# One gather of 8 KB per expert in place of two of 4 KB, in a hybrid encoder with product-key experts

## The reference

```python
def one_block(hb):                                   # 128 tokens
    q = (hb @ w_query).reshape(t, 8, 2, 128)         # 8 heads, two halves
    s = einsum('thpc,phkc->thpk', q, keys)           # 128 keys per half
    sv, si = top_k(s, 16)                            # 16 best of each half
    ...                                              # 256 sums, the 16 best of them
    idx  = ...                                       # 8 x 16 = 128 experts per token
    gate = softmax(top_s)
    u = expert_u[idx]                                # 128 rows of 1024 per token
    act = gelu(einsum('tnd,td->tn', u, hb))
    return einsum('tn,tnd->td', gate * act, expert_v[idx])
```

## Time and profile before

| | us |
|---|---|
| median of 3 runs | 3242.87 |
| lowest and highest run | 3241.06, 3247.12 |
| the profiled execution: its time | 3239.72 |
| its span, first to last instruction | 3237.8 |

### The profile page before, as it was taken

The page is one execution under the profiler, slowest core; times in us unless marked ns, Lnnn a source line. Parts: engine busy times, 40 slices in busy tenths (PEclk is TensorE's granted clock), DMA queues, the critical chain, the costliest instruction groups (busy, mean ns, idle before and its releaser), DMA issues.

```text
span 3237.8 us, 29913 instructions
## 1 busy us (share of the span) xinstructions
PE 2408.2 (74%) x5786; PEld 1028.4 (32%) x5796; DVE 2227.9 (69%) x5353; ACT 465.2 (14%) x1379; POOL 2073.9 (64%) x2147
## 2 busy tenths in 40 slices
PE   7999986876677567756677677767776777766557
PEld 3575342332233223323233233323332333222113
DVE  1123178897679867975689669866887679866663
ACT  1126211111111111101111111111111111111000
POOL 0000125677777777767767777777777777777775
PEclk9999998998899999989998989988998899888999
DMA  3121148999999999999999999999999999999999
GB/s 105 52 112 57 33 130 315 388 396 398 409 409 405 396 407 409 401 408 408 409 379 399 401 401 409 376 401 401 408 376 401 401 409 410 408 402 399 409 410 364
DMA packets 319943, 1134.32 MB, mean 350 GB/s; under 512 B 37825, under 2 KB 42945, under 8 KB 317793
## 3 DMA queue, kind: packets, MB, share of 16 engines
q0 software_dynamic: 299520, 1090.65, 85.6%
q1 hardware_dynamic: 20320, 42.62, 3.6%
HBM read 1130.97 MB, written 2.10 MB: 350 GB/s over the span
## 4 chain that ended last, share of the span: by engine, by line
DMA 24%; issue 20%; DVE 17%; PE 14%; POOL 6%; DVEq 1%; ACT 1%; POOLq 0%; ACTq 0%
DMA v_ring<-in_peer_v,idx_v 21%; PE psum L1370 12%; DVE u_ring L1462 4%; DMA u_ring<-in_peer_u,idx_u 3%; POOL u_ring L1339 3%; POOL v_ring L1351 3%; DVE hres L1454 2%; DVE work L1101 1%; PE psum L975 1%; DVE si L1117 1%; DVE si L1099 1%; DVE sv L1126 1%; DVE tpos L1099 1%; DVE sv L1111 1%; DVE tpos L1117 1%
## 5 line engine op out<-in xcount | busy, mean ns | idle before, releaser
L1370 PE MATMUL psum<-v_ring,w_col 128*128 128x512 f32 x3136 | 1681.8, 673 | 760.3 <-DMA v_ring<-in_peer_v,idx_v 662.3
L1462 DVE SCALAR_TENSOR_TENSOR u_ring<-u_ring,psum 128x1024 f32<-128x1024 f32 x1040 | 1255.5, 1215 | 525.2 <-DMA u_ring<-in_peer_u,idx_u 467.7
L1339 POOL DMA_INDIRECT u_ring<-in_peer_u,idx_u x1040 | 1032.4, 993 | 468.1 <-issue 269.3
L1351 POOL DMA_INDIRECT v_ring<-in_peer_v,idx_v x1040 | 1025.6, 986 | 340.1 <-issue 266.0
L1370 PEld LDWEIGHTS psum<-v_ring,w_col 128*128 128x128 f32 x3136 | 613.8, 211 | 1739.2 <-issue 1333.1
L1454 DVE SCALAR_TENSOR_TENSOR hres<-v_ring,weight,hres 128x1024 f32 (+1 forms) x256 | 328.1, 1282 | 37.4 <-DMA v_ring<-in_peer_v,idx_v 28.7
L1418 ACT ACTIVATE w_col<-ident,weight 128x128 f32<-128x128 f32 x768 | 247.8, 391 | 125.5 <-DVE weight L1447 111.9
L975 PE MATMUL psum<-wq,hbT 128*128 (+1 forms) x512 | 249.6, 601 | 4.0 <-DVE work L1101 2.7
L1403 ACT ACTIVATE ge<-ga 128x16 f32<-128x16 f32 x65 | 14.0, 215 | 1589.7 <-DVE ga L1435 1589.7
L460 POOL IOTA iota<- 128x16 f32 x1 | 0.1, 144 | 336.5 <-ACT catT L745 336.5
L975 PEld LDWEIGHTS psum<-wq,hbT 128*128 128x128 f32 x512 | 98.4, 194 | 131.2 <-issue 129.8
(11 more groups left out here) (225 smaller groups left out, 1479.4 us busy)
## 6 DMA issues: line engine op xcount, KB each, us to landing
u_ring<-in_peer_u,idx_u POOLq DMA_INDIRECT x1040, 9.1
v_ring<-in_peer_v,idx_v POOLq DMA_INDIRECT x1040, 9.1
wq<-in_peer_w_query SPq DMA_DIRECT2D x16, 1024.0 KB, 19.7
w_ring<-in_even_w_in SPq DMA_DIRECT2D x6, 2048.0 KB, 7.9
w_ring<-in_even_w_out SPq DMA_DIRECT2D x1, 4096.0 KB, 14.2
hres<-in_x SPq DMA_DIRECT2D x4, 512.0 KB, 5.4
out<-hres SPq DMA_DIRECT2D x1, 2048.0 KB, 6.6
hbT<-in_peer_sub_keys SPq DMA_DIRECT2D x6, 256.0 KB, 11.2
```

Of the source, the lines that this page charges most:

```text
L1339: nc.gpsimd.indirect_dma_start(u_ring[:, i % U_SLOTS, :], None, u_rows, bass.IndirectOffsetOnAxis(idx_u[par][:, i:i + 1], 0)).then_inc(s_u ...
L1351: nc.gpsimd.indirect_dma_start(v_ring[:, i % V_SLOTS, :], None, v_rows, bass.IndirectOffsetOnAxis(idx_v[par][:, i:i + 1], 0)).then_inc(s_v ...
L1370: ins = nc.tensor.matmul(y_ps[:, half, :], w_col[:, n % W_SLOTS, :], v_ring[:, i % V_SLOTS, 512 * half:512 * half + 512], start=False, sto ...
L1462: nc.vector.scalar_tensor_tensor(out=row, in0=row, scalar=1.0, in1=rows, op0=ALU.mult, op1=ALU.mult, accum_out=dot[par][:, i:i + 1]).then_ ...
```

## The change

**One gather per slot.** Outside the kernel the two tables are joined into rows of 8 KB, once as U then V (`peer_uv`) and once as V then U (`peer_vu`). The cells are laid out in six groups of three: V, U, V. A gather of a V-U row fills the first two cells of a group, the next gather into the same group fetches U-V and fills the last two. So the group has one U cell and two V cells. `Place` works out, for each row, its group, its side, and the two conditions before the gather: `dotted`, the dot of the row before it in the group, and `summed`, the sum of the row two before it. Four of the groups (`ring_early`) lie where nothing of the mixer does, two (`ring_late`) can be used when the mixer's last projection is done. `TILE_ORDER` gives the groups within a tile: rows 0 to 83 go round all six, rows 84 to 103 round five, rows 104 to 127 round six.

**Weights per eight.** The gelu argument is formed after each eight dots (three instructions, where there were four), and the weights are made after the first dot of the next eight. U and V of a slot now arrive together, so V is no longer two chunks behind.

**Sums.** All 16 slots of a chunk go through TensorE, with 8 buffers of `w_col`. `add_vector` and `take_sum` are gone. TensorE opens a tile's sum with the residual (`open_sum`, identity times residual), and ACT copies the finished sum back (`take_scalar`) in the next tile, after its column 3; `open_sum` of that tile waits for this copy.

**Keys and the rest.** The keys come transposed from outside, in one load per layer. The gates' constants (`bands`) are made later on POOL, the selections of pieces 2 and 3 of the first tile move behind the start of the sums, the projections use two PSUM banks in turn, the loops over pairs of chunks are written out as whole tiles, the hooks stand at new slots, and the output goes out tile by tile. The descriptor space of the gathers goes from 8192 to 4096 bytes.

```diff
+GROUPS_EARLY, GROUPS_LATE = 4, 2
+META_ORDER = [0, 1, 2, 3, 0, 1, 2, 3, 4, 5, 0, 1, 2, 3, 4, 5]
+TILE_ORDER = [g for _ in range(14) for g in range(6)] + [g for _ in range(4) for g in range(5)] + [g for _ in range(4) for g in range(6)]
...
+        self.dotted = rows[-1] + 1 if len(rows) > 0 else None
+        self.summed = rows[-2] + 1 if len(rows) > 1 else None
...
-                    wait(pool, s_dot, CHUNK * u + i + 1 - U_SLOTS)
-                    nc.gpsimd.indirect_dma_start(u_ring[:, i % U_SLOTS, :], None, u_rows,
-                    nc.gpsimd.indirect_dma_start(v_ring[:, i % V_SLOTS, :], None, v_rows,
+                at = Place(j, i if j is None else CHUNK * c + i)
+                if at.dotted is not None:
+                    pool.wait_ge(s_dot, at.dotted)
+                if at.summed is not None:
+                    pool.wait_ge(s_acc, at.summed)
+                apart(pool)
+                nc.gpsimd.indirect_dma_start(pair_cells(at), None, uv_rows if at.side else vu_rows,
...
+        def columns_scalar(act, j, c, base, hooks=()):
+            for i in range(CHUNK):
+                m = QUADS * u + i // QUAD
+                if i % QUAD == 0:
+                    act.wait_ge(s_garg, m + 1)
+                    wait(act, s_weight, m)
+                    nc.scalar.activation(ge[:, :], ga[:, :], ACT.Exp, scale=-GELU_B).then_inc(s_gexp, 1)
+                    act.wait_ge(s_weight, m + 1)
+                if j is not None:
+                    act.wait_ge(s_acc, CHUNK * u + i + 1 - W_SLOTS)
...
-                if i == 3 and not first:
-                    gelu_weights(dve, u - 1, 1 - par)
-                if dst is not None and i and on_vector(i - 1):
-                    add_vector(dve, u - 2, par, i - 1, dst)
+                if i % QUAD == 0 and q > 0:
+                    gelu_weights(dve, u, m - 1, par, q - 1)
+                elif i == 0 and j is not None:
+                    gelu_weights(dve, u - 1, m - 1, 1 - par, QUADS - 1)
+                if i % QUAD == QUAD - 1:
+                    dve.wait_ge(s_dot, CHUNK * u + i + 1)
+                    gelu_argument(dve, m, par, q)
...
+        def open_sum(pe, j):
+            for half in range(2):
+                if j is not None:
+                    pe.wait_ge(s_yadd, 2 * j + 1 + half)
+                nc.tensor.matmul(y_ps[:, half, :], ident[0:n, :], rows[:, 512 * half:512 * half + 512],
+                                 start=True, stop=False, skip_group_check=True)
+        def take_scalar(act, j):
+            act.wait_ge(s_acc, CHUNK if j is None else CHUNK + TILE_ROWS * (j + 1))
+            for half in range(2):
+                nc.scalar.copy(rows[:, 512 * half:512 * half + 512], y_ps[0:n, half, :]).then_inc(s_yadd, 1)
...
+        TOOK, TURNED, TURN_TOOK, SCORE, SORT = 3, 4, 7, 8, 15
+        QUERIED = (7, 27, 47, 67)
...
+            return [(1, lambda: keep_scalar(act, j + 2, CHUNK + TILE_ROWS * j)), (TAKE, lambda: take_scalar(act, j - 1))]
...
-    nc = bacc.Bacc("TRN2", target_bir_lowering=False, num_devices=1, dynamic_dma_scratch_size=8192)
+    nc = bacc.Bacc("TRN2", target_bir_lowering=False, num_devices=1, dynamic_dma_scratch_size=4096)
```

More of the change, by code:

```diff
@@ L1736, in _ @@
+            def iteration(j, layer, start=()):
+                dve.wait_ge(s_hd, j + 2)
+                tile(j, routing_vector(dve, j + 2) + tables_hooks(dve, j + 2, layer, 96) + list(start))
             dve.wait_ge(s_meta_rows, 1)
[L1737 to L1738 removed]
+            stages = topk_stages(dve, first_piece(1) + 1, 1, P)
+            dots_vector(dve, None, 0, meta_rows.rearrange("p a b -> p (a b)"),
+                        [(1 + i, stages[i]) for i in range(TOPK_STAGES)] +
+                        [(14, lambda: piece_indices(dve, 1)), (15, lambda: piece_gates(dve, 0))])
@@ L1792, in _, with tile @@
             first_query(1)
-            for i in range(6, 2 * TILES):
+            for i in range(7, 2 * TILES):
                 project_tensor(pe, i)
-            first_query(2)
-            first_query(3)
-            def pair(j, s, first=(), second=()):
-                v = TILE_CHUNKS * j + 1 + 2 * s
-                experts_tensor(pe, v, first)
-                experts_tensor(pe, v + 1, second)
-            def iteration(j, start=(), keys=()):
-                open_sum(pe, j + 1)
-                with pe.Fori(0, 2) as s:
-                    pair(j, s, *routing_tensor(pe, j + 2, s))
-                pair(j, 2, (), keys)
-                pair(j, 3, *start)
-                close_sum(pe)
+            def tile(j, hooks):
+                open_sum(pe, j)
+                for c in range(TILE_CHUNKS):
+                    sums_tensor(pe, j, c, of_chunk(hooks, c))
```

648 lines of the change are left out of this document (292 added, 356 removed).

## The result

| | before | after |
|---|---|---|
| median of 4 runs, us | 3244.43 | 3818.28 |
| lowest and highest | 3241.06, 3247.12 | 3813.30, 3822.81 |
| ratio, 95% interval | | 1.177 (1.175 to 1.179) |
| span of the profiled execution, us | 3237.8 | 3812.8 |
| mean granted clock of TensorE over that span | 0.93 | 0.87 |

The change makes the kernel 17.7% slower. I had said 3572 us and at most 3700: the direction is right, the size is not. The changed kernel took 3824, 3813 and 3828 us in three later sets of runs. In two other sets the kernel before took 3652 and 3621 us, at a mean granted clock of 0.85 to 0.86 in place of some 0.92; the changed kernel was not timed in those two, no trace shows them, and the cause is open.

A forecast was written before the change was run, and what follows sets the result against it. Transfers (402 GB/s) bound the kernel before, the ring of 12 V cells the changed one. Per tile 331.8 + 12.5 + 21.6 + 7 + 4.4 = 377 us; 519 + 3018 + 30 = 3567, forecast 3572, range 3190 to 3700.

The forecast's parts named there:

- What bounds, and what changes: Middle of the kernel: transfers bound it before; after, DMA share about 0.87, 355 GB/s, POOL waiting for sums, clock under 0.85.
- T, the transfer of one slot: Gathers: a slot of 8 KB rows takes 2.49 us at 422 GB/s, bounds 2.41 and 2.56.
- Rival 4: Gathers: 8 KB rows move no faster, 2.56 us per slot; forecast rises by 40 us, inside the range, no separate chance.
- The chain: V ring, landing of slot k + 8 to that of k + 12: dot, weights, sum, wake and landing take 10.8 us.
- The cold clock: TensorE's bursts: half clock after idling costs 2.7 us in 8 of 16 eights, 21.6 us per tile, bounds 0 and 43.
- plain eight: Eight slots of a tile with TensorE warm: 10.8 + 4 x 2.49 = 20.7 us, 331.8 us per tile.
- Hooks and the edge: Per tile: DVE's selections wait 7 us for key scores, and PE's opening of the tile waits 4.4 us.
- Rival 2: Tiles: the V ring binds and the rest is hidden, 3303 us, up to 3400 with smaller terms; chance 0.25.
- five groups: Rows 84 to 103 of a tile: V cells return after 10 or 11 slots, costing 12.5 us per tile.
- Start and end: Outside the tiles: tile 0's first landing near 519 us, and 30 us from the last landing to the end.
- 1 (transfers win): Tiles: the steps between landings fit under 9.96 us and TensorE stays warm, 3120 to 3200 us; chance 0.18.
- 3 (TensorE falls behind): TensorE's sums: idling and half clock feed each other, 470 us per tile, over 4000 us; chance 0.06.

The follow-up runs named there:

- Experiments 1 and 2: On the changed kernel: 1, sums read a fixed operand and no gather waits for a sum, 3239 us; 2, 16 rounds of five groups instead of 4, 4146 us.
- weights per four: Changed kernel with four slots instead of eight sharing one making of weights: 3181, 3183 and 3180 us, ratio 0.981 to the kernel before.
- experiment 5: Changed kernel with TensorE multiplying zeros in idle gaps, three tries: five in a row, 3865 us; spread over the gap, 3871; spread and behind the hooks, 3733.
- experiment 6: ACT's copy of the finished sum put ahead of the new tile's first exponential: 3800 us on the changed kernel, 3181 with weights per four.
- first try: Changed kernel with five multiplications by zeros in a row on TensorE after nine of a tile's sixteen eights: 3865 us.

## Why the prediction was wrong in size

**What bounds, and what changes: right.** The rate of 402 GB/s was the bound, it fell to 332 (I had said 355), and the mean clock to 0.87 with 0.85 in the middle (said under 0.85). POOL waits for sums (by the count gather by gather, above), PE works in bursts of 32 matmuls, share of the DMA engines 0.85 (said 0.87). Experiments 1 and 2 show the mechanism, not only its signs.

**T, the transfer of one slot: right, with luck.** With weights per four six or seven of the last tile's sixteen eights take 19.9 us, 8 x 2.49. But the stretch from which I read 422 GB/s, 232 to 246 us, holds 441 packets of 4 KB beside 498 of 8 KB, so it did not show 8 KB rows alone. Rival 4 is out.

**The chain: right in its sum, off in its items.** Plain and cold I had 10.8 + 2.7 + 9.96 = 23.4 us; the row by row sum is 23.43, and the mean of the plain eights 23.7. The landing is 5.77 from POOL's start (5.45 in the sum; 5.4 to 5.8 in nine rounds of that tile), and after the dry queue the four landings take 10.74 us instead of 9.96: rows 3533.18 and 3536.13 come 2.8 and 2.95 us after the one before. In the nine rounds the four take 10.7 to 11.8. Against that, dot to weights takes 1.83 for 2.0 and the cold sum 3.74 where the forecast had it at 3.75 and the second one late by 0.9 besides. In this round the second gather goes out 1.7 us after the first, so the 0.9 is not there. The misses cancel, and that the sum hits is in part luck. A warm eight took 21.1 for 20.7.

**The cold clock: the step that failed.** "I count 8 of 16" was an assumption about the trace after, and the trace after has 12 to 14 of 16 in tiles 1 to 6, 13 in the mean, and 15 in the last (granted clock in the first 1.5 us of each burst). With my 2.7 each that is 13.5 us more per tile than I took. What one cold start costs is less sure than how many there are: experiment 5 gives 1.9 us, while the eights that began warm by themselves (21.1 us) lie 2.6 under the cold ones (23.7). At 1.9 the count adds only 3 us to my 21.6 (13 x 1.9 = 24.7), and 17 us go to the plain eight instead, which would then take 21.8 warm for my 20.7. I had reasoned that query products keep PE busy through their eight. They do, but what counts is the gap ahead of the next burst: it is short only where products or scores stand at the end of an eight. In tiles 1 to 6 the burst began at full clock after every gap of 0.2 to 2.3 us, at one or the other after gaps of 3.0 to 3.8, and at 0.50 to 0.62 after all gaps of 4 us and more. I had even written the bound, 43 us for all cold, and then didn't carry it into the range: 3572 + 8 x 21.4 = 3743.

**Hooks and the edge: the second miss.** For both I had 7 + 4.4 = 11.4 us. A tile with hooks (periods summed, tiles 1 to 6) takes some 410 us, 14 to 16 more than the last tile, though three of its bursts are warm (6 to 8 us less): so the hooks and the edge cost 20 to 24. The edge is 5.9 us in the trace where I had 4.4: I had priced the opening warm, 0.9 us, and it ran at half clock, 3.6. DVE's wait for scores is 61 us in six tiles, 10 per tile, where I had 7. The rest, 4 to 8 us per tile, is not traced to one wait. Rival 2 had it that a late ring hides such delays. It hides a part at most: of the 5 us that experiment 6 took from a tile's second eight, 3.4 stayed in the tile's time.

**The sum again.** 377 + 13.5 (cold) + 9 to 13 (hooks and edge) + 16 x 0.3 (plain eight) + 0.9 (five groups) = 405 to 409, of the 410.5 measured. The hooks' term is itself a difference of measured tiles, so the sum says how the error divides and is no second proof. One tile, the third, took 425: around 1604 to 1618 us its landings come 4.5 to 5 us apart while the second layer's keys and query weights come in on SP's queue (22.7% of the DMA time from 1590 to 1650 us, the gathers 67.6%), which I hadn't looked at.

**Start and end.** The first gather went out at 425.6 instead of 433, tile 0's first row was there 4.5 us late, and the end took 23.4 us instead of 30: together 2 us less than foretold. All 248 us of the span's error are in the tiles.

**Rivals.** 1 (transfers win) asked for a chain under 9.96 us; it was 12.7 between the two landings. By the Trainium skill (DMA: Bandwidth & Descriptors, Anatomy of one DMA) a DMA that POOL issues takes about 2.0 us plus its bytes over 436 GB/s, for a gather of 1 MB an estimated 4.4 us. The trace shows 5.77 here and no less than 5.4 in nine rounds, so it disagrees. 3 (TensorE falls behind) did not happen: each burst was back at full clock after one to two sums.

## What to carry to other kernels

When a buffer is filled earlier than its reader can use it, count in slots how long it is held, and compare that with the ring before looking at anything else: here eight slots of waiting plus a chain of 12.7 us in a ring of 12 lost 17.7%, and four slots of waiting won 1.9%. Once a ring binds, most of what its chain contains counts, the clock after idle time too (3.4 of 5 us in experiment 6, 1.4 of 1.9 in experiment 5), so take such costs at their upper bound and let the range reach the sum of them. Filling idle time is only free if nothing small and urgent stands behind the filler.

## What the runs showed of the hardware

- Gathers of 8 KB rows moved a little faster than gathers of 4 KB rows on one core: 411 GB/s over 2000 us against 402, and 421 to 422 in the best slices of weights per four and of experiment 1 against 409 to 410 in those of the kernel before. At best a slot took 2.49 us. The number of gathers halves with it, so it isn't shown that the row length alone does it.
- After the queue had run dry, the second and third gather (issued 1.7 us apart) landed 2.8 and 2.95 us behind the one before instead of 2.47. I had not expected such a cost beyond the first landing; for the four landings of a round it was 0.8 us there, and 0.7 to 1.9 in nine rounds of the last tile, 1.2 in the mean.
- In the changed kernel TensorE's clock was at or near its lower level (0.50 to 0.62 granted) at the start of every burst after idle 4 us or more, 12 to 14 of 16 bursts in tiles 1 to 6, and in the last tile of experiment 5 a filler that ended 0.4 us ahead of the burst kept it at the upper one. The gap alone doesn't decide: in that experiment's first try two bursts began at 0.88 after 4.1 and 4.2 us.
